# A shift vector multiplied by TensorE, and a pooled stage with its product ahead of the window sums

## What is computed

```python
def ada_modulation(c, w, b):
    mod = jax.nn.silu(c) @ w + b
    shift, scale, gate = jnp.split(mod, 3, axis=-1)
...
        shift, scale, gate = ada_modulation(c, ada_w[layer, 0], ada_b[layer, 0])
        h = rms_norm(x, norm_w[layer, 0]) * (1.0 + scale) + shift
```

```python
def multiscale_pool_mixer(h, pool_w, pool_scale):
    cs = jnp.cumsum(hf, axis=1)
    for gi, w in enumerate(POOL_WINDOWS):
        lag = jnp.pad(csg, ((0, 0), (w, 0), (0, 0)))[:, :S]
        cnt = jnp.minimum(t + 1, w).astype(jnp.float32)[None, :, None]
        pooled = (csg - lag) / cnt - hf[..., lo:hi]
        outs.append(pooled.astype(h.dtype) @ pool_w[gi])
    return jnp.concatenate(outs, axis=-1) * pool_scale
```

## Time and profile before

| | us |
|---|---|
| median of 3 runs | 957.27 |
| lowest and highest | 956.63 and 958.1 |
| the profiled execution | 958.09 |
| its span, first to last instruction | 956.4 |
| PE busy | 888.4 |
| DVE busy | 692.1 |
| ACT busy | 456.8 |

### The profile page before, as it was taken

How to read it: one execution, slowest core, us unless ns; L and a number is a source line. 1 busy time by engine, 2 the same in 40 slices (tenths; PEclk the granted TensorE clock), 3 DMA queues, 4 the chain that set the end, 5 groups by cost and what they waited for, 6 DMA issues and landing times.

```text
span 956.4 us, 17671 instructions
## 1 busy us (share of the span) xinstructions
PE 888.4 (93%) x7028; PEld 852.6 (89%) x7028; DVE 692.1 (72%) x877; ACT 456.8 (48%) x573; POOL 58.0 (6%) x104
## 2 busy tenths in 40 slices
PE   2599999899999996799999999999999999999996
PEld 1388879799999996699999999988989999999996
DVE  4889878788878888766666556855487877776665
ACT  2347464566643333456663433444465444444445
POOL 2110110211111110000000000000000000000000
PEclk9789999999999996799999999999999999999998
DMA  9895755499989994057765555653435555654531
GB/s 336 300 339 193 244 200 177 130 319 322 317 306 330 330 316 134 23 184 234 239 199 176 175 183 168 197 166 130 157 90 177 177 179 187 218 173 158 169 126 44
DMA packets 156600, 196.60 MB, mean 206 GB/s; under 512 B 5341, under 2 KB 143116, under 8 KB 156556
## 3 DMA queue, kind: packets, MB, share of 16 engines
q1 hardware_dynamic: 142732, 145.64, 47.6%
q0 software_dynamic: 13824, 50.34, 14.4%
HBM read 194.90 MB, written 1.06 MB: 205 GB/s over the span
## 4 chain that ended last, share of the span: by engine, by line
PE 81%; DVE 9%; ACT 4%; issue 2%; DMA 2%; SPq 1%; DVEq 0%; ACTq 0%
PE G L557 15%; PE G L558 15%; PE G L559 15%; PE A L557 7%; PE A L559 7%; PE A L558 7%; DVE w_lo L1123 2%; ACT w_hi L1786 2%; PE G L632 2%; PE A L685 2%; PE G L633 2%; PE G L634 2%; DMA sinks<-in_attn_sinks_dram 1%; DMA MIX<-bias_rows 1%; DVE HN L1285 1%
## 5 line engine op out<-in xcount | busy, mean ns | idle before, releaser
L1123 DVE TENSOR_TENSOR w_lo<-raw,w_hi 128x2048 fp32r<-128x2048 f32 x135 | 307.1, 2275 | 163.7 <-ACT w_hi L1786 163.5
L1786 ACT ACTIVATE w_hi<-raw 128x2048 fp32r<-128x2048 f32 x135 | 256.6, 1901 | 265.7 <-PE A L559 132.4
L557 PE MATMUL G<-h_hi,w_hi 128*128 128x256 f32 x880 | 257.9, 293 | 22.5 <-DVE h_lo L1268 13.0
L558 PE MATMUL G<-h_lo,w_hi 128*128 128x256 f32 x880 | 253.3, 288 | 0.0
L559 PE MATMUL G<-h_hi,w_lo 128*128 128x256 f32 x880 | 253.2, 288 | 0.0
L557 PEld LDWEIGHTS G<-h_hi,w_hi 128*128 128x128 f32 x880 | 173.0, 197 | 29.5 <-issue 22.5
L558 PEld LDWEIGHTS G<-h_lo,w_hi 128*128 128x128 f32 x880 | 173.6, 197 | 0.2 <-issue 0.2
L559 PEld LDWEIGHTS G<-h_hi,w_lo 128*128 128x128 f32 x880 | 173.2, 197 | 0.0
L557 PE MATMUL A<-u_hi,w_hi 128*128 128x256 f32 x512 | 143.4, 280 | 0.7 <-DVE w_lo L1123 0.7
L558 PE MATMUL A<-u_lo,w_hi 128*128 128x256 f32 x512 | 142.9, 279 | 0.0
L559 PE MATMUL A<-u_hi,w_lo 128*128 128x256 f32 x512 | 142.9, 279 | 0.0
(11 more groups left out here) (325 smaller groups left out, 1315.7 us busy)
## 6 DMA issues: line engine op xcount, KB each, us to landing
raw<-in_mlp_w_dram SPq DMA_DIRECT2D x64, 1024.0 KB, 5.5
ada_raw<-in_ada_w_dram POOLq DMA_DIRECT2D x88, 512.0 KB, 5.7
raw<-in_w_in_dram SPq DMA_DIRECT2D x14, 1024.0 KB, 5.0
raw<-in_w_up_dram SPq DMA_DIRECT2D x11, 1024.0 KB, 5.4
raw<-in_w_gate_dram SPq DMA_DIRECT2D x11, 1024.0 KB, 5.3
raw<-in_attn_w_in_dram SPq DMA_DIRECT2D x9, 1024.0 KB, 7.1
raw<-in_w_down_dram SPq DMA_DIRECT2D x8, 1024.0 KB, 5.2
raw<-in_attn_w_out_dram SPq DMA_DIRECT2D x4, 1024.0 KB, 5.4
```

Source lines behind the costliest of these rows:

```text
L557: pe.matmul(dst, wh, ah, start=start, stop=False)
L558: pe.matmul(dst, wh, al, start=False, stop=False)
L1123: dve.tensor_tensor(w_lo[n % 2][:, 0:k, :], raw[n % RAW][:, 0:k, :], w_hi[n % 2][:, 0:k, :].bitcast(F32), ALU.subtract).then_inc(lo_done, 1)
L1786: act.activation(w_hi[n % 2][:, 0:k, :], raw[n % RAW][:, 0:k, :], ACT.Copy).then_inc(hi_done, 1)
```

## The change

It does five things.

1. The shift of m = 0 isn't added up by VectorE. Its eight pieces are loaded into buffers that attention uses only later (`shift_w`), and PE multiplies each with the column of silu(c) (`shift_tile`, eight products of one column), all into one bank. VectorE keeps eight additions before the first norm.
2. `rel_bias` is loaded third and the table is made first; the write of the table stands ahead of three small loads, its reading back (`hankel`) behind `g_raw` and ahead of the first block. The gate pieces of m = 0 are loaded after the second block. `n0` is written into a buffer of its own for all eight tiles, ahead of the shift.
3. All transposes for the sums are gone: `add_sums` takes one, two or three thirds of a modulation at once. Between `up(0)` and `down(0)` it now takes three (gate 1, shift 2, scale 2) and waits for all 56 additions; before it took gate 1 and waited for all but the last two.
4. In `down(0)` the halves of X times the gain of m = 2 are made tile by tile (L1631 of the new program, two for each pass), as `down(1)` did before for its own successor. The last of four passes is written out: it has four more operations on VectorE and on ACT for the pool's weights times shift and scale (`sw_part`, `sw_ready`), and it adds its last two `ada_pair` ahead of the two residual tiles, where before they came after them.
5. In the pooled stage the product with the pool's weights comes first, with tokens on the partitions; the norm's root and the shift's part go on in `z_tok`; then PE multiplies with a band matrix over tokens (`band`, `band2`, made by VectorE after `up(0)`), 16 products of 144 and 128 columns.

```diff
+            def shift_tile(k):
+
+                pe.wait_ge(shift_full[k], 16)
+                for t in range(DT):
+                    last = pe.matmul(shift_dst[:, t:t + 1], shift_w[k][:, t * P:(t + 1) * P],
+                                     c_silu[:, k:k + 1], start=k == 0 and t == 0, stop=k == DT - 1,
+                                     skip_group_check=True)
+                return last
...
-            turn_sums(0, "scale", DT)
+            shift_tile(1)
             pe.wait_ge(table_in, 16)
             for q in range(4):
                 dst = bank_empty(pe, f"flip{q}")
                 bank_done(f"flip{q}", pe.matmul(halves(dst), anti, hankel[:, 2 * q:2 * q + 2, :],
                                                 start=True, stop=True))
-            turn_sums(0, "shift", 2 * DT)
+            shift_tile(2)
+            shift_tile(3)
+            add_sums("scale0", ((0, SCALE),), DT)
+            for k in range(4, DT):
+                last = shift_tile(k)
+            bank_done("shift0", last)
...
-            turn_sums(0, "gate", ADA_B)
...
+            add_sums("gate0", ((0, GATE),), ADA_B)
             for j in range(4):
                 feature_block(N_OUT + j, 9 + j, split="mix0" if j == 0 else None,
...
-            scale_and_shift(1)
+            add_sums("sums1", ((1, SHIFT), (1, SCALE)), ADA_C)
...
             up(0)
-            add_sums(1, "gate", ADA_D - 2)
+            add_sums("sums2", ((1, GATE), (2, SHIFT), (2, SCALE)), ADA_D)
             down(0)
-            add_sums(2, "scale", ADA_D)
-            mean_square(2)
-            add_sums(2, "shift", ADA_D)
-            add_sums(2, "gate", ADA_E)
...
+            pool_group(0)
+            pool_group(1).then_inc(pool_done, 1)
+            pool_group(2)
+            token_sums("ms2", 2)
+            pe.wait_ge(sw_ready, 1)
+            for p in range(2):
+                pe.wait_ge((down_free0, down_free1)[p], 5)
+                dst = bank_empty(pe, f"sw{p}")
+                bank_done(f"sw{p}", pe.matmul(halves(dst), ones[:, :], HN[p][:, :, :], start=True, stop=True))
+            add_sums("gate2", ((2, GATE),), ADA_E)
+            pool_group(3).then_inc(block_used, 1)
...
-            scale_and_shift(3)
+            add_sums("sums3", ((3, SHIFT), (3, SCALE)), ADA_E)
...
-            turn_sums(3, "gate", 96)
+            add_sums("gate3", ((3, GATE),), ADA_ALL)
```

More of the change, by code:

```diff
@@ L43, in first_block @@
 def first_block(t):
-    return (1, 0, 2)[t // DT], t % DT
+    return (1, 2)[t // DT], t % DT
 SHIFT, SCALE, GATE = 0, 1, 2
[L51 to L55, removed]
+ADA_B, ADA_C, ADA_D, ADA_E, ADA_ALL = 16, 32, 56, 80, 88
+ADA_EARLY = (3, 4, 5, 6, 7, 11, 12)
+ADA_SLOT = [1 if f >= ADA_E else f % 3 for f in range(ADA_ALL)]
+ADA_LOADS = [sum(ADA_SLOT[e] == ADA_SLOT[f] and e not in ADA_EARLY for e in range(f + 1)) for f in range(ADA_ALL)]
 def ada_before(f):
@@ L1102, in _ @@
                 if ks[0] == 0:
[L1103 to L1109 removed]
+                    token_sums("ms7", 7)
             turn_rows(3)
@@ L1184, in modulation @@
             def modulation(m):
-                chain(part(m, "scale"))
-                factor(m)
-                part(m, "shift").then_inc(mod_ready, 1)
-                dve.wait_ge(mod_ready, m + (m < 2))
+                thirds(f"sums{m}", m, SHIFT, 2)
+                factor(m).then_inc(mod_ready, 1)
+                dve.wait_ge(mod_ready, {1: 1, 3: 2}[m])
             ssq = [0]
@@ L1388, in _ @@
             scaled(0, 0)
+            ada_next(1)
             biased(0, 1)
@@ L1397, in _ @@
             scaled(0, 1)
-            chain(part(0, "gate"))
             biased(0, 2)
@@ L1521, in mlp, with out_tiles @@
                 start = chain.count
-                with dve.Fori(0, 4) as i:
-                    chain.looped = i * 2
+                def out_tiles(i, last):
+                    chain.looped, chain.count = i * 2, start
                     done = 0
@@ L1592, in _ @@
-            part(2, "gate")
+            for p in range(2):
+                if p == 0:
+                    dve.wait_ge(pool_done, 1)
+                else:
+                    dve.wait_ge(block_used, N_POOL + 1)
+                bank_was_read(dve, f"sw{p}")
+                for k in range(2):
+                    u = U_POOL + 2 * p + k
+                    dve.scalar_tensor_tensor(out=z_tok[:, k, 512 * p:512 * p + 512], in0=G[u % 4][:, :],
+                                             scalar=t_rstd[:, k:k + 1], in1=sw[:, p, :], op0=ALU.mult,
+                                             op1=ALU.add).then_inc(g_free[u % 4], 1)
```

396 lines of the change are left out of this document (214 added, 182 removed).

## The result

The changed kernel takes 989.91 us (median of four executions, 989.3 to 994.11) against 957.68 beside it: ratio 1.0346, interval 1.0316 to 1.0377, so slower by 32.2 us. The forecast was 980, with a range of 960 to 992. The profiled execution took 990.02, its span is 988.3 (before 956.4).

A forecast was written before the change was run, and what follows sets the result against it. TensorE was taken as the bound, nearly without a wait outside the opening and the pooled stage. The terms, 12 - 0.9 + 1.0 + 2.5 + 16.9 + 0.5 - 10 + 0.8 = +22.8 on 957.3, gave 980 us, range 960 to 992.

The forecast's parts named there:

- 1, opening: Up to the first block's end: later table and flips, then slim shift products, two groups fast and five slow; +12 us.
- 2, gate 0: Gate 0: eight transposes go, -0.9 us; eight slim products ahead of the first output block, VectorE waiting, +1.0.
- -0.9 of the transposes: Gate 0: the eight transposes at 76.4 us go, saving 0.9 us.
- 3, sums 1: Sums 1: 16 slim products replace 16 transposes ahead of the mean square, and the clock may fall; +2.5 us.
- 4, sums 2: Between up(0) and down(0): PE idles 5.6 us for the last addition, then 24 products at 1.2 GHz; +16.9 us.
- 4, the rest, down(0): down(0): VectorE's band operations make a low half late, plus two halves of X in each pass; +0.5 us.
- 5, the stage: Pooled stage: VectorE's norm and windows go, PE's own path is the next bound; -10 us.
- 6, gate 3: Gate 3: eight transposes become eight slim products; +0.8 us.
- Rival A: Wherever slim products stand: they keep or raise the clock; +3.9 us, 961; chance 0.20.
- B: Sums 2: the clock does not fall in the wait before it; faster, -4.3 us, 953; chance 0.06.
- C: Everywhere around the slim products the clock stays low; 995 us; chance 0.12.
- D: Pooled stage: z_tok waits longer, VectorE's windows stay on the path, eating some of -10; inside the forecast's 0.58.

The follow-up runs named there:

- a_open: Changed kernel with the opening of the kernel before (shift of m = 0 added up by VectorE, old order of loads): 975.3 us.
- a_fat: Changed kernel with 128 columns of ones, not one, in every add_sums product; the shift stays at one column: 980.3 us.
- a_both: Changed kernel with up(0)'s additions spread 2, 2, 2, 0 and 128 columns in all add_sums products: 979.0 us.
- a_2220: Changed kernel with the six additions of each up(0) pass spread 2, 2, 2, 0 instead of 2, 1, 2, 1: 989.5 us.
- a_order: Changed kernel with the last weight block's halves made ahead of X's halves in the first three passes of down(0): 990.4 us.
- a_pad: Changed kernel with the unused 32-byte buffer part_sums back in its old place, so buffers behind it lie 32 bytes higher: 989.0 us.
- a_wide: Changed kernel with 128 columns in add_sums products and the shift's 64 products written 64 columns wide: 975.6 us.

## Why the prediction was right, and where it was off

**Direction and mechanism were right, the size was 9 to 10 us short** (+22.8 forecast, +32.2 measured). 989.9 lies in the range of 960 to 992, but beyond the 971 to 989 that the forecast gave itself, and the terms missed nearly all to one side, so the range held by its width. Term by term:

- **1, opening: +12 forecast, 10.3 at the end of the first block.** The table came back at 33.7 (32.3), the flips ended at 39.2 (38.3), the shift stood at 58.3 (59.8), the first block started at 60.6 (62) and ended at 68.5 (70). Three groups were fast and four slow, two and five were forecast. a_open gives 12 for the opening as a whole. That the hit is so close is in part luck: the start of block 9's high half, 135.35 here, lies between 131.3 (a_fat) and 141.2 (a_both) in kernels whose opening is the same but for the columns of scale 0.
- **2, gate 0: +0.1 net forecast, 3.1 measured: mis-sized.** The step "VectorE waits for them with two low halves queued behind" was right, but the products ran 3.0 us, not 1.8, because the clock fell within them (153.6), and it stayed down over most of the output block behind (to 160.4). The -0.9 of the transposes is in the first row of the table and doesn't show there: a new wait of 1.5 us for VectorE in the attention took its place.
- **3, sums 1: +2.5 forecast, 4.3 measured.** The bound was 3.5. The products took 4.29 for 3.7, so 2.2 more than the transposes. The other 1.9 is the mean square behind them, which ran wholly at the low clock (3.8 us for 1.9). The idle 4.1 us that follows is the same in both kernels.
- **4, sums 2: +16.9 forecast, 15.7 measured.** Wait 5.67 (5.6), products 10.4 (10.7). Right in place, releaser and size. The reason given for the clock, the idle stretch, was half the truth: here it did fall in it (290.1), but a_2220 shows that the products of one column bring it down with 1.5 us of wait, and a_both that this wait alone doesn't.
- **4, the rest, down(0): +0.5 forecast, 3.9 measured.** "The two halves of X in each pass" stood within the +0.5, without a working of its own. ScalarE and VectorE have the room for them; but a half that waits, put ahead of one that is ready, makes the ready one late (1.6 us by a_order). The other 2.3 are position.
- **5, the stage: -10 forecast, -10.4 measured at the squares' sum** (25.3 for 35.7), and -9.4 at block 48.
- **6, gate 3: +0.8 forecast, 1.1 measured.**
- **No term: 2.5 us in down(1) and behind, and 2.3 in down(0), from 32 bytes.** A removed buffer counted as free. Together it was the largest single miss, 3.8 to 4.8 us: mended alone in a_pad, it gave back 1.3 of the 2.3 in down(0).

Rival A, slim products that keep the clock, is refuted by the changed kernel itself and by a_wide. B fell with it (its sum also leaves out term 4's +0.5; with it, 953.5). C had the right feature, more slow stretches than the forecast took, and at 995 lay nearer to the measurement in that. D did not happen: `z_tok` stood at 413.7, and waited 1.1 us. The forecast's two tests for being wrong (first block before 52, no wait at sums 2) both came out for it.

## What to carry to other kernels

When a sum or a turn goes to TensorE as a product of one column, give it more columns: eight products cost 1.84 us with one column and 2.03 with 128 (a_fat, at 43.66 and 41.80), and the clock held over the wide ones at sums 2 in a_both. The Trainium skill, "TensorE: Matmul & The Clock Gate", section "LDWEIGHTS (loading the stationary operand)", has the weight load go by the columns of the weights; the nearly equal prices here agree. Before a sum is made to wait for the last piece of a loop, look what the last piece is queued behind; and never put a half that waits ahead of one that is ready. After any change of buffers, compare the time of one untouched block in both traces: it tells in a line whether the memory's layout has moved the whole kernel.

## What was not expected of the hardware

- TensorE's clock fell from 2.4 to 1.2 GHz in gapless work of one-column products (changed kernel at 44.4, busy without a gap since 33.74), and in six other kernels with the same shift at 42.8 to 47.0. It didn't in the same work at 64 columns (a_wide).
- When it falls differs where the opening is the same (42.8 us in a_both, 47.0 in a_fat), and the high half behind the first norm came 7.6 us later in the one than in the other. A profile is one draw.
- Back to back products of 256 columns in float32 step by 0.120 us with the moving operand on a multiple of 64 bytes and by 0.1167 at 32 bytes past one. Moving the activations of the kernel before by 32 bytes, with the loads' and the small buffers beside them and nothing else, gives 1.0% (0.7 to 1.3).
